# Scores of the next pair of heads issued ahead in the third layer's attention loop, with one constant product a unit instead of two

## The reference

```
q, kc, vc, ks, vs, kw, vw, gl, z = split_cols(u @ w_in, A_SPLITS)
kcmp = compress(kc, pos_k, w1_k, w2_k)        # 15 compressed keys: gelu(blk @ w1) @ w2
vcmp = compress(vc, pos_v, w1_v, w2_v)
o_c = masked_softmax(q @ kcmp - slope * dist) @ vcmp      # branch 1: compressed
o_s = masked_softmax(q @ ksel - slope * dist) @ vsel      # branch 2: selected blocks
o_w = masked_softmax(q @ kwin - slope * dist) @ vwin      # branch 3: window
o = sum(gates * [o_c, o_s, o_w])
y = (o * silu(z)) @ w_out
```

## Time and profile before

| | |
|---|---|
| median of 3 runs | 1999.64 us (1998.54 to 2002.29) |
| the profiled execution | 2000.51 us, of which its span is 1998.7 us |
| mean granted TensorE clock | 0.946 of full speed |
| PE busy | 1760.1 us, 88% of the span |
| DVE busy | 1134.2 us, 57% |
| ACT busy | 979.5 us, 49% |
| the loop of the change | about 1366 to 1470 us from the span's start |

### The profile page before, as it was taken

How to read it: one execution, slowest core, us unless ns; L and a number is a source line. 1 busy time by engine, 2 the same in 40 slices (tenths; PEclk the granted TensorE clock), 3 DMA queues, 4 the chain that set the end, 5 groups by cost and what they waited for, 6 DMA issues and landing times.

```text
span 1998.7 us, 25505 instructions
## 1 busy us (share of the span) xinstructions
PE 1760.1 (88%) x10032; PEld 1383.9 (69%) x10032; DVE 1134.2 (57%) x1875; ACT 979.5 (49%) x1738; POOL 102.2 (5%) x135
## 2 busy tenths in 40 slices
PE   5997879995899974898899998987899989999987
PEld 2775547673777754666799997765677757777866
DVE  2115984445788865764566667435755375445454
ACT  4223225624788855464344333643546465635563
POOL 0000100002000002100000002000000000000000
PEclk8998889998899996999899999998999999999998
DMA  8345785012999972202255554442025404514521
GB/s 311 127 187 190 281 301 227 1 64 105 376 421 421 422 295 106 95 1 85 91 186 187 188 189 168 151 145 85 1 73 191 167 22 158 190 43 161 189 82 43
DMA packets 52694, 335.89 MB, mean 168 GB/s; under 512 B 5488, under 2 KB 5488, under 8 KB 18288
## 3 DMA queue, kind: packets, MB, share of 16 engines
q1 hardware_dynamic: 46112, 310.04, 41.0%
q0 software_dynamic: 6480, 24.44, 3.2%
HBM read 305.10 MB, written 29.36 MB: 167 GB/s over the span
## 4 chain that ended last, share of the span: by engine, by line
PE 69%; DVE 12%; ACT 9%; DMA 5%; issue 3%; POOL 1%; SPq 0%; POOLq 0%; DVEq 0%; ACTq 0%
PE bank L1314 18%; PE bank L1316 17%; PE bank L1315 17%; DMA ring_float<-weights_dram 3%; PE bank L1347 2%; ACT arena_float L831 1%; DVE ring_float32r L2235 1%; ACT ring_high L696 1%; PE bank L1568 1%; ACT hT_float L744 1%; PE bank L1529 1%; PE bank L1694 1%; PE bank L1742 1%; PE bank L1686 1%; PE bank L1974 1%
## 5 line engine op out<-in xcount | busy, mean ns | idle before, releaser
L2235 DVE TENSOR_TENSOR ring_float32r<-ring_float,ring_high 128x1024 fp32r<-128x1024 f32 x298 | 355.7, 1231 | 368.6 <-ACT ring_high L696 368.4
L696 ACT ACTIVATE ring_high<-ring_float 128x1024 fp32r<-128x1024 f32 x298 | 302.1, 1059 | 411.3 <-DMA ring_float<-weights_dram 408.5
L1314 PE MATMUL bank<-ring_high,x_float32r 128*128 128x512 f32 x608 | 242.1, 398 | 7.8 <-DVE mix_float32r L2274 5.1
L1315 PE MATMUL bank<-ring_float32r,x_float32r 128*128 128x512 f32 x608 | 238.7, 393 | 0.0
L1316 PE MATMUL bank<-ring_high,mix_float32r 128*128 128x512 f32 x576 | 226.4, 393 | 0.0
L1314 PE MATMUL bank<-ring_high,arena_float32r 128*128 128x512 f32 (+1 forms) x368 | 141.7, 385 | 14.4 <-DVE arena_float32r L2264 6.6
L1314 PE MATMUL bank<-Z_float32r,ring_high 128*128 128x256 f32 x512 | 145.1, 283 | 7.2 <-issue 4.2
L1315 PE MATMUL bank<-Z_float32r,ring_high 128*128 128x256 f32 x512 | 145.2, 284 | 0.0
L1316 PE MATMUL bank<-Z_float32r,ring_float32r 128*128 128x256 f32 x512 | 145.1, 283 | 0.0
L1314 PEld LDWEIGHTS bank<-ring_high,x_float32r 128*128 128x128 f32 x608 | 114.1, 188 | 41.8 <-issue 7.4
L1315 PE MATMUL bank<-ring_float32r,arena_float32r 128*128 128x512 f32 (+1 forms) x368 | 139.1, 378 | 0.0
(11 more groups left out here) (420 smaller groups left out, 3334.6 us busy)
## 6 DMA issues: line engine op xcount, KB each, us to landing
ring_float<-weights_dram SPq DMA_DIRECT2D x234, 1024.0 KB, 4.8
Z_float<-weights_dram SPq DMA_DIRECT2D x33, 1024.0 KB, 8.7
sent<-post_row SPq DMA_DIRECT2D x1, 11776.0 KB, 37.5
Z_float<-sent SPq DMA_DIRECT2D x23, 512.0 KB, 9.1
made<-mix_float POOLq DMA_DIRECT2D x23, 512.0 KB, 7.9
post_row<-norm_post_dram POOLq DMA_DIRECT2D x4, 512.0 KB, 4.3
small<-small_dram SPq DMA_DIRECT2D x1, 1072.0 KB, 9.0
x_float<-x_dram SPq DMA_DIRECT2D x1, 1024.0 KB, 5.2
```

Of the source, the lines that this page charges most:

```text
L696: nc.scalar.activation(ring_high[:, slot, half], ring[:, slot, half], ACT.Copy).then_inc(high_ready, 1)
L1314: nc.tensor.matmul(out, left[0], right[0], start=start, stop=False)
L1315: nc.tensor.matmul(out, left[0], right[1], start=False, stop=False)
L2235: ve.tensor_tensor(ring_low[:, slot, half], ring[:, slot, half], ring_high[:, slot, half], ALU.subtract).then_inc(low_ready, 1)
```

## The change

In this loop alone:

- The scores get four banks: a new pool `C` on banks 2 to 5 in place of `SC` on 4 and 5. The turns and the side work, before in pool `A` (banks 0 to 3), go to the existing pool `PT` on banks 0 and 1.
- `attend` has a new argument `ahead`. With `ahead=2` the scores of units 0 and 1 are issued ahead of the loop, and at each even step those of units step + 2 and step + 3 in place of step and step + 1. The side work stays ahead of them in the step.
- One constant product a unit in place of two.
- The compressed scores are still issued at units 10 and 16 on PE, but DVE and ACT take them at 12 and 18; their product with the values goes from 15 and 21 to 17 and 23 on all three engines.
- PE waits for all of `A` ahead of the loop, and for all of `PT` and `C` ahead of `turn_first`. `first_block` waits for `C` instead of `SC`.

```
-CMP_SCORE, CMP_PROBS, CMP_OUT = (10, 16), (13, 19), (15, 21)
+CMP_SCORE, CMP_SOFT, CMP_PROBS, CMP_OUT = (10, 16), (12, 18), (15, 21), (17, 23)
+        C = Banks(bank[2:6], c_full, c_free)
...
+                for u in range(0, ahead, 2):
+                    score(u)
                 for step in range(n_u + lead + 1):
                     if step < n_u and not (paired and step % 2):
                         if between:
                             between(step)
                             if paired:
                                 between(step + 1)
-                        score(step)
+                        if step + ahead < n_u:
+                            score(step + ahead)
                     if lead <= step < n_u + lead:
                         u = step - lead
                         seen.next(lag_events)
                         b = turned.take(pe)
-                        for _ in range(DENSE_PAIRED if paired else filler):
+                        for _ in range(min(filler, DENSE_PAIRED) if paired else filler):
...
+                A.drained(pe)
                 def score(u):
-                    banks = [SC.take(pe) for _ in range(2)]
+                    banks = [C.take(pe) for _ in range(2)]
...
+                def last():
+                    PT.drained(pe)
+                    C.drained(pe)
+                    turn_first()
                 attend(LT * 16, score, ..., weigh, probs_ready,
-                       between=compressed, paired=True, last=turn_first)
+                       between=compressed, paired=True, turned=PT, filler=1, last=last,
+                       ahead=2)
```

More of the change, by code:

```diff
@@ L834, in pT_out, with pt_drain @@
                 drain((pT_ring[u % 3][:, 0:width], lambda b, w=width: b[:, 0:w], 1.0, None))
+            def pt_drain(dst, width):
+                b = PT.filled_bank(act)
+                nc.scalar.activation(dst, b[:, 0:width], ACT.Copy).then_inc(pt_free, 1)
             def pT_pair_out(u, width):
@@ L1191, in compressed @@
                                                          b[32 * g:32 * g + 32, hk * 64:(hk + 1) * 64], ACT.Copy)
-                        n.then_inc(a_free, 1)
-                    if u in CMP_SCORE:
+                        n.then_inc(pt_free, 1)
+                    if u in CMP_SOFT:
                         seen.next(cmp_in)
@@ L1200, in compressed @@
                         for half in range(2):
-                            drain((cmp_rows[:, qt, half * 512:(half + 1) * 512], lambda b: b[:, :], 1.0, None))
-                        whole["cmp", qt] = A.drains
+                            pt_drain(cmp_rows[:, qt, half * 512:(half + 1) * 512], 512)
+                        whole["cmp", qt] = PT.drains
                 n_u = LT * 16
@@ L1511, in head_features, with attend @@
                     i.then_inc(a_full, 1)
-            def attend(n_u, score, turn, weigh, lag_events, lead=2, between=None, paired=False, turned=A, filler=DENSE, last=None):
+            def attend(n_u, score, turn, weigh, lag_events, lead=2, between=None, paired=False, turned=A, filler=DENSE, last=None,
+                       ahead=0):
                 pT_at = {}
+                for u in range(0, ahead, 2):
+                    score(u)
                 for step in range(n_u + lead + 1):
@@ L2016, in compressed @@
                             if h >= 14:
-                                i.then_inc(s_full, 1)
+                                i.then_inc(c_full, 1)
                     if u in CMP_PROBS:
                         seen.next(cmp_probs)
-                        b = A.take(pe)
+                        b = PT.take(pe)
                         for hk in range(4):
                             i = nc.tensor.transpose(b[:, hk * P:(hk + 1) * P], cmp_p[:, hk * P:(hk + 1) * P], ident)
-                        i.then_inc(a_full, 1)
-                        fills["probs"] = A.fills
+                        i.then_inc(pt_full, 1)
+                        fills["probs"] = PT.fills
                     if u in CMP_OUT:
-                        A.drained(pe, fills["probs"])
+                        PT.drained(pe, fills["probs"])
                         for half in range(2):
-                            b = A.take(pe)
+                            b = PT.take(pe)
                             for hk in range(2):
@@ L2980, in compressed @@
                         gelu(1)
-                    if u in CMP_SCORE:
-                        qt = CMP_SCORE.index(u)
+                    if u in CMP_SOFT:
+                        qt = CMP_SOFT.index(u)
                         dve.wait_ge(late_loaded, 16)
                         for odd in range(2):
-                            b = SC.filled_bank(dve)
+                            b = C.filled_bank(dve)
                             dst, bias = (v.rearrange("p (h o n) -> p h o n", o=2, n=CMP_N)[:, :, odd, :] for v in (cmp_s, cmp_bias[:, qt, :]))
-                            then(ve.tensor_tensor(dst, b[:, 0:120].rearrange("p (h n) -> p h n", h=8), bias, ALU.add), s_free)
+                            then(ve.tensor_tensor(dst, b[:, 0:120].rearrange("p (h n) -> p h n", h=8), bias, ALU.add), c_free)
                         then(ve.tensor_reduce(rsum[:, 0:16], sc, AX.X, ALU.max))
                         signal(ve.tensor_tensor(sc, sc, over(rsum[:, 0:16], CMP_N), ALU.subtract), cmp_in)
-                    if u - 1 in CMP_SCORE:
-                        qt = CMP_SCORE.index(u - 1)
+                    if u - 1 in CMP_SOFT:
+                        qt = CMP_SOFT.index(u - 1)
                         seen.next(cmp_out)
@@ L2998, in compressed @@
                         if qt > 0:
-                            dve.wait_ge(a_free, whole["cmp", qt - 1])
+                            dve.wait_ge(pt_free, whole["cmp", qt - 1])
                         signal(ve.tensor_tensor(cmp_p.rearrange("p (h n) -> p h n", h=16)[:, :, 0:CMP_N], sc,
@@ L3021, in out @@
                     cmp = cmp_rows[:, qt, h0 * HD:(h0 + 4) * HD].rearrange("p (h d) -> p h d", h=4)
-                    dve.wait_ge(a_free, whole["cmp", qt])
+                    dve.wait_ge(pt_free, whole["cmp", qt])
                     for first, branch_rows in ((cmp, w[:, :, 0, :]), (dst, w[:, :, 1, :])):
@@ L3033, in sparse @@
                     if u == 16 + 5:
-                        dve.wait_ge(a_free, whole["cmp", 0])
+                        dve.wait_ge(pt_free, whole["cmp", 0])
                         then(ve.tensor_tensor(mix[:, 0, :], mix[:, 0, :], cmp_rows[:, 0, :], ALU.add))
```

45 lines of the change are left out of this document (23 added, 22 removed).

## The result

The changed kernel takes 1985.12 us (median of 7 runs, 1982.75 to 1992.29), the kernel before 2000.51 us in the same comparison (1997.62 to 2006.57): a ratio of 0.9924, 95% interval 0.9907 to 0.9941, or 15.4 us less. The forecast was 16.0 us less, to 1983.6. Repeated beside the first experiments the ratio was 0.9932 (0.9919 to 0.9946).

The account below looks back on a forecast made before the run. It took a ring through PE, DVE and ACT, no single engine, to bound the loop. Second half 11, first half 4.6 and end 0.4 sum to 16.0 us less, 1999.64 to 1983.6 us; 8-in-10 range 1975.5 to 1993.

Parts of the forecast that it names:

- The third: Last two units, where PE runs without waits: fewer constant products save 0.4 us.
- The ring: In the loop, a pair's scores wait for the previous pair's weighing (5.24 us of durations); scores ahead cut this.
- Second half: Loop from 1411 to 1463: of 52 us, 14 at most can go, less some 3 for waits: 11 us gained.
- waits for each other: Second half: some 3 us guessed for DVE and PE waiting at each `out` and piece of side work.
- Equal load: Second half: DVE and PE come out nearly equal at 38 us.
- First half: Loop from 1374 to 1411: 4.6 us gained, between 0 and 15, as ACT's sixteen copies and the low clock stay.
- the slower rival: Whole loop: less constant work with pauses left lets the clock sit at 1.2 GHz; +24 us, 2023.6, chance 0.05.
- Constant products: Loop: 6.9 us less PE time at full clock, no gain of its own; without it PE needs 40 us in second half.
- DVE alone as the bound: Whole loop: DVE's waits for scores and compressed scores go; -28 us, 1971.6, chance 0.13.
- Rival 2: Loop: stalls move to the two banks and ACT; first half gives nothing, second half of its 14; -7 us, chance 0.2.
- The signs: Loop: DVE's score waits under 8 us, second half 40 to 42 with DVE over 0.9 busy, first half 31 to 34.
- The clock rule: PE in the loop: small pauses between matmul groups can make the clock swing, speaking against halving constant work; would give 2023.6.

Follow-up runs that it names:

- the first experiments: The first follow-up runs, timed beside the kernel before; the changed kernel, repeated unedited beside them, had ratio 0.9932.
- two_constants: Changed kernel with two constant products a unit, as before, instead of one; ratio 0.9963 to the kernel before.
- banks_alone: Changed kernel with no scores issued ahead and the compressed softmax at its old units; ratio 1.0017 to the kernel before.
- clock_hold: Changed kernel with extra constant products: 9 at unit 1, 8 at unit 5, 6 at unit 6; ratio 0.9929 to the kernel before.
- all_three_more: The kernel of all_three with 4 more constant products at units 6 and 7; 1979.53 us, ratio 0.9887 to the kernel before.
- again: The changed kernel once more, without an edit; ratio 0.9932 to the kernel before.
- kv_one_bank: Changed kernel with both second compression products of unit 8 in one bank instead of two; ratio 0.9928 to the kernel before.
- four_copies: Changed kernel with ACT's sixteen small copies of unit 8 made as four of 32x256; ratio 0.9917 to the kernel before.
- all_three: Changed kernel with clock_hold (without its products at unit 6), kv_one_bank and four_copies together; 1978.40 us, ratio 0.9896 to the kernel before.
- less_vector: Changed kernel without DVE's sum of the first row tile with the compressed branch; ratio 0.9926 to the kernel before.
- no_constants_second: Changed kernel with no constant product at units 16 to 31; ratio 0.9913 to the kernel before.
- one_constant_alone: The kernel before with one constant product a unit in this loop and nothing else changed; ratio 1.0021 to the kernel before.

## Why the prediction was right

It was right in time and, for the second half, in mechanism. Two of its three terms were mis-sized in opposite directions, so that the sum came within 0.6 us of the measured time is in part luck. (The third, 0.4 us at the end, was 0.2.)

- *The ring.* That the wait between weighing and scores sets the pair's time was right: taking it away with everything else kept (two_constants against the kernel before) gives 7.4 us, and all edits but that one (banks_alone) give nothing. The later compressed softmax changes with the order in both of these, as said above.
- *Second half, forecast 11 us.* Measured 13.0 and 13.9. The ceiling of 14 us was right, with DVE at 37.9 to 38.8 us; the 3 us that I took off as "waits for each other" were a guess, and they hardly exist: in this half the profiles list one wait of DVE in the first, of 0.8 us and for ACT, and none in the second. The 0.9 us between the two go with the clock: with scores ahead and one constant in this half, the profiles with 0.96 (the first, clock_hold, all_three_more) have 38.8 us, those with 1.00 (**again**, kv_one_bank, four_copies, all_three) 37.9. That the three units of slack in `s_ring` take up an `out` of 2.7 us is my explanation; no run tested it.
- *Equal load.* That DVE and PE would both be at 37 to 38 us held: less work for DVE gives 0.3 of 1.22 us (less_vector), less for PE gives nothing (no_constants_second), more for PE (6.9 us of constants over the loop, half of them here) lengthens half and tail by 3.7 us together, against **again**.
- *First half, forecast 4.6 us.* Measured 1.5 and 3.5. The step that failed is above all the clock ahead of unit 8: I assumed the low stretches of the trace before, 1392 to 1403 above all, and worked unit 8 at full clock. In the first profile the low level began 9 us after the loop's start and stayed for some 26 us (0.50 in the window below), so unit 8's product took 3.63 us instead of 1.95, and the sixteen copies began 2.3 us later than before instead of 0.3 earlier. clock_hold removes most of it and gives 4.8 to 6.7 us in its profile, though the timed runs don't show it as time. This is the place where the slower rival had a part, in the first half only. The window, of the first profile of the changed kernel:

```profile
1380.00:1385.00 5.00, 5.00 (x26) 5.00 (x24) 3.16 (x6) 1.29 (x7) 0.00 (x0) 0.50 0.00 0
```

A second slip has nothing to do with the clock. I let the compressed scores follow PE's pause at once, from 1392.0. Between them stands a weighing, before and after (the kernel before first, then the second profile of the changed one):

```profile
1392.08 1.11 PE L2058 MATMUL bank<-Z_float,hT_float 128*128 128x64 f32 x4 [2.56 <-ACT hT_float L662]
1393.12 3.60 PE L2013 MATMUL bank<-Z_float,arena_float 64*128 64x15 f32 x32
```
```profile
1393.11 1.12 PE L2070 MATMUL bank<-Z_float,hT_float 128*128 128x64 f32 x4 [0.62 <-ACT hT_float L846]
1394.16 3.60 PE L2024 MATMUL bank<-Z_float,arena_float 64*128 64x15 f32 x32
```

In all three profiles these scores begin 2.4 us after the end of the sixteen copies. So even in the second profile, whose unit 8 ran at full clock, the copies began 0.4 us later than before, counted from the loop's start, and the scores of units 12 and 13 behind the compressed ones only 0.7 us earlier; I had 0.3 and 2.0 us earlier.

- *Constant products.* "Not a gain of its own" holds in the old order, where taking one away costs 4 us; with scores ahead taking one of the two away is worth 6.2 us by the timed runs (some 2 to 10), more than the 3 us that I had between 40 and 37.
- *The other rivals.* DVE alone as the bound (-28) is refuted by the first half, 43.3 and 41.3 us with DVE busy 27.6, and in the second half by less_vector. Rival 2 has its sign: ACT waits 9.7 us for turns, over the 8 that I had named, 6.0 of them in the first half. But the loss it stands for did not come in the second half, and at unit 8 the two banks are not the reason: kv_one_bank needs one bank less there and nothing changes. The other places where side work takes banks were not tested.
- *The signs.* DVE's wait for the scores was to fall under 8 us: 9.0 in the first profile, 6.6 in the second. The second half was to be 40 to 42 us with DVE over 0.9 busy: it is 38.8 and 37.9 with 0.94 and 0.96. The first half was to be 31 to 34 us, counted from 8 us after the loop's start: it is 35.3 and 33.4.
- *The clock rule.* The Trainium skill's warning in "TensorE: Matmul & The Clock Gate", section "A second HAM failure mode: psum-queue depth-cycling", that small pauses between groups make the clock swing, agrees with one_constant_alone (0.85 over the second half) and not with the second half of the changed kernel (0.96 and 1.00), where the pauses themselves are gone.

Open is how much the clock's place costs from run to run: the loop differs by 2.8 us between two profiles of one kernel. That the 6.2 us of two_constants are more than the 3.7 us of its longer half and tail was not followed up either; its profile is of one of its fastest executions.

## What to carry to other kernels

Where a pair of units waits in a ring through three engines, look first at the place in the issue order and then at the buffers: a free bank behind the wrong instruction gave nothing, the same bank with the next unit's work issued ahead gave the whole gain. Constant work that keeps the clock up pays only while there are pauses around it. When the pauses go it turns from a help into load, so its amount is set again after each change of the order; in the profiles it did most when placed in the pauses themselves. And where two engines come out equally loaded with some units of buffer between them, the work of the busier one was the time here, without a deduction for waits.

## What the runs showed of the hardware

- In no_constants_second PE was busy 28.4 of 30 us with a granted clock of 1.00; a pause of 1.1 us followed, and from 1447 us the clock was 0.54. At that level eight weighing products took 1.81 instead of 1.00 us, and in the two profiles of the changed kernel the 16 small products of unit 8 took 3.63 instead of 1.95.
- In the first half of the first profile of the changed kernel PE paused 2.13 and 2.21 us with some 0.9 us of work between; the granted clock was 0.50 right after. With 17 constant products in these two pauses (clock_hold) it stayed at 1.00 there.
- ACT's copies of 32x64 take 0.225 us each (16 in 3.60), those of 32x256, four times as large, 0.38 each (4 in 1.53).
- One edit, one constant product less a unit, changed the time by +4 us (2 to 6) and by -6 us (some -2 to -10) in two orders of the same loop.
